# Hybrid decoder layer on one core: feed-forward operands stored as sums, three up products run in the output projection's phase, one DVE addition moved

## Chip, core and metric
One core of a Trainium2 chip runs the whole layer in one launch. The metric is device time in microseconds (us) of that launch; the median of several runs is compared. Everything is float32, and every large matmul is computed as three matmuls on operands split into a high and a low part (fp32r).

## What is computed
`x` is (1, 2048, 1024). The token-mixing half comes first (RWKV-7 recurrence and causal pooling); its result is `mixed_in`, and the change begins at its output projection. Cut to what matters:

```python
mixed = mixed_in @ w_out                              # 1024 x 1024
x = x + rms_norm(mixed, post_mix_norm)
h = rms_norm(x, pre_ffn_norm)
up = h @ w_up                                         # 1024 x 5632
up = causal depthwise conv over time (width 3) + conv_b
gate, val = split(up, 2)
f = (gelu_tanh(gate) * val) @ w_down                  # 2816 x 1024
x = x + rms_norm(f, post_ffn_norm)
```

## The kernel before
The kernel has four phases, one after the other, each a block with its own program for the five engines: input projection, recurrence, output projection (`phase_mix_out`, L1804) and feed-forward (`phase_ffn`, L2101). At the end of a phase all engines meet; a small block that sets semaphores (`credit`) stands between two.

**The products.** Up and down projection are multiplied by Strassen's method in Winograd's form: the operand is cut in four quarters, A11 to A22, four sums S1 to S4 are made of them, and seven products P1 to P7 replace eight. P1 is `ph` 0, P7 is `ph` 6. Of the eight quarters and sums seven are operands (`OPERANDS`); `OPERAND` is their place in memory. Each product of one weight tile is 4 x 3 = 12 matmuls (`split_matmul`, L130: L132, L133, L134).

**Output projection.** Sixteen tiles of 128 rows, written out (`tiles`). TensorE does tile t's 48 matmuls and then the eight transposes of tile t-1 (L2078). For each tile ScalarE squares the result (L1979), DVE scales it (L2050) and adds it to x (L2054), ScalarE squares x, DVE takes a reciprocal, ScalarE writes `xs` (L1992), which TensorE turns. DVE's `turn` (L2014) puts the turned tile into `quarter`; two tiles give one set of quarters, and `sums` (L2028) makes S1 to S4. ScalarE copies quarters and sums to high parts (L1952, L1959), GpSimd (L1927) and DVE (L2043) subtract them to get the low parts, and ScalarE's queue stores both parts in the memory tensors `q_hi` and `q_lo` (L1954, L1961, L1965, L1969). SyncE (SP) loads the mixed tiles and x, and behind the last tile the first three operands of the first superblock (L1910, L1911).

**Feed-forward.** Two superblocks of 1024 rows. In each, 22 units (one 128-wide gate tile and one value tile each) do the up projection. Units 0, 1, 20 and 21 are written out, the others are a hardware loop over pairs. In unit n ScalarE and DVE also split the weights of unit n+1 (`high` L2482, `low` L2638); GpSimd makes the weight sums `tsum` (`sums` L2415: L2425, L2427, L2430, L2434), in the first superblock also sums of down weights (`piece_sums` L2436), and sums of the hidden values of two units (`pair_sums` L2448, first line L2452), which wait for the hidden values (`hidden` L2670: DVE's product of gate and value, L2680). PSUM has four banks a unit; `BANK` says which product uses which, P4 goes onto P1's bank (after ScalarE's copy, L2494) and P7 onto P5's, after DVE's addition `add(n, 2, 4, ...)` (L2649 is the line of all additions). The order of DVE's steps in a unit is that of `unit` (L2722); in it `hidden(n - 1)` stands just ahead of `add(n, 2, 4, ...)`.

Then come 77 steps of the down projection (`step`), a ring of three buffers, split by L2533 (ScalarE) and L2684 (DVE). In the first superblock's steps SP also loads the next superblock's operands, high and low, in 56 parts. At the start of the phase SP loads the convolution parameters (L2348 to L2350), two weight tiles (L2291), operands 3 to 6 in high and low parts (L2310) and the last norm's gain (L2358).

Of the kernel before, what the change touches and what calls it, by code (L numbers as in the profile page):

```python
# [14 lines left out]
P = 128  # L15
# [33 lines left out]
OPERAND = (0, 4, 3, 1, 5, 6, 2)  # L49
EARLY_OPERANDS = 3  # L50

# [1752 lines left out]
def phase_mix_out(nc, a, scr):  # L1804
    ctx, sems = ExitStack(), []
    with ctx:
# [17 lines left out]
        m_lo = [scr["m_lo0"], scr["m_lo1"]]  # L1824
        x = two("x", [P, D_MODEL])
        hs = [sb("hs", [P, D_MODEL])] * 2
        xs = two("xs", [P, D_MODEL])
        sq = [sb("sq", [P, D_MODEL], mybir.dt.bfloat16)] * 2

        quarter = sb("quarter", [P, 8, KQ, P])  # L1830
        q_hi = sb("q_hi", [P, OPERANDS, KQ, P], F32R)
        q_lo = sb("q_lo", [P, OPERANDS, KQ, P], F32R)
# [25 lines left out]
        s_hh = sem("quarters_hi_ready")  # L1858
        s_hle = sem("first_quarters_lo_ready")
        s_hll = sem("last_quarters_lo_ready")  # L1860
        s_she = sem("first_quarters_hi_stored")
        s_shl = sem("last_quarters_hi_stored")
        s_sle = sem("first_quarters_lo_stored")
        s_sll = sem("last_quarters_lo_stored")
        s_pre = sem("first_operands_loaded")

        xv = a["x"][0].rearrange("(t p) d -> t p d", p=P)

# [9 lines left out]
        def place_of(q):  # L1878

            at = q // 4 * TB + q % 4 * P  # L1880
            return slice(at, at + P)

        credit(nc, sems)
        with nc.Block() as block:
            @block.sync
            def _(sp):
# [8 lines left out]

                def body(t, p):
# [8 lines left out]
                    if t == N - 1:  # L1905

                        for s in (s_she, s_shl, s_sle, s_sll):
                            sp.wait_ge(s, ONE + N // 4 * 16)
                        for ph in range(EARLY_OPERANDS):
                            sp.dma_start(scr["o_hi"][ph][:, :, :].bitcast(F32), scr["q_hi"][:, OPERAND[ph], :, 0:TB]).then_inc(s_pre, 16)  # L1910
                            sp.dma_start(scr["o_lo"][ph][:, :, :].bitcast(F32), scr["q_lo"][:, OPERAND[ph], :, 0:TB]).then_inc(s_pre, 16)  # L1911

                tiles(body)
                sp.wait_ge(s_pre, ONE + 32 * EARLY_OPERANDS)
                for p in range(2):
                    sp.wait_ge(s_sx[p], ONE + N * 8)
                for s in (s_she, s_shl, s_sle, s_sll):
                    sp.wait_ge(s, ONE + N // 2 * 16)

            @block.gpsimd  # L1920
            def _(gp):
                nc.gpsimd.memset(eps[:, :], NORM_EPS).then_inc(s_const, 1)

                def first_low(q):
                    gp.wait_ge(s_hh, ONE + 2 * q + 1)
                    gp.wait_ge(s_sle, ONE + q * 16)
                    nc.gpsimd.tensor_tensor(q_lo[:, 0:2, :, :], quarter[:, 0:2, :, :], q_hi[:, 0:2, :, :].bitcast(F32), ALU.subtract).then_inc(s_hle, 1)  # L1927

                def body(t, p):
                    if t < N - 2:  # L1930
                        gp.wait_ge(s_mh, ONE + t + 3)
                        nc.gpsimd.tensor_tensor(m_lo[p][:, :, :], m_raw[p][:, :, :], m_hi[p][:, :, :].bitcast(F32), ALU.subtract).then_inc(s_ml, 1)
                    if p == 1:
                        first_low(t // 2)


                gp.wait_ge(s_ml, ONE + 2)
                tiles(body)

            @block.scalar  # L1940
            def _(act):
# [6 lines left out]
                def first_high(q):  # L1948

                    act.wait_ge(s_h, ONE + 2 * q + 1)  # L1950
                    act.wait_ge(s_she, ONE + q * 16)
                    nc.scalar.activation(q_hi[:, 0:2, :, :], quarter[:, 0:2, :, :], ACT.Copy).then_inc(s_hh, 1)  # L1952
                    act.wait_ge(s_hh, ONE + 2 * q + 1)
                    act.dma_start(scr["q_hi"][:, 0:2, :, place_of(q)], q_hi[:, 0:2, :, :].bitcast(F32)).then_inc(s_she, 16)  # L1954

                def last_high(q):
                    act.wait_ge(s_sum, ONE + 4 * q + 4)
                    act.wait_ge(s_shl, ONE + q * 16)
                    nc.scalar.activation(q_hi[:, 2:OPERANDS, :, :], quarter[:, 3:8, :, :], ACT.Copy).then_inc(s_hh, 1)  # L1959
                    act.wait_ge(s_hh, ONE + 2 * q + 2)  # L1960
                    act.dma_start(scr["q_hi"][:, 2:OPERANDS, :, place_of(q)], q_hi[:, 2:OPERANDS, :, :].bitcast(F32)).then_inc(s_shl, 16)  # L1961

                def store_first_low(q):
                    act.wait_ge(s_hle, ONE + q + 1)
                    act.dma_start(scr["q_lo"][:, 0:2, :, place_of(q)], q_lo[:, 0:2, :, :].bitcast(F32)).then_inc(s_sle, 16)  # L1965

                def store_last_low(q):
                    act.wait_ge(s_hll, ONE + q + 1)
                    act.dma_start(scr["q_lo"][:, 2:OPERANDS, :, place_of(q)], q_lo[:, 2:OPERANDS, :, :].bitcast(F32)).then_inc(s_sll, 16)  # L1969

# [4 lines left out]
                def body(t, p):  # L1975
# [3 lines left out]
                    nc.scalar.activation(sq[p][:, :], bank[:, 2 * p:2 * p + 2, :].rearrange("p b d -> p (b d)"), ACT.Square,  # L1979
# [6 lines left out]
                    nc.scalar.activation(sq[p][:, :], x[p][:, :], ACT.Square, accum_out=ss[p][:, 1:2]).then_inc(s_sq, 1)  # L1986
# [3 lines left out]
                    if t > 1:  # L1990
                        act.wait_ge(s_tr, ONE + t - 1)
# [973 lines left out]
```

## Time and profile before

| | us |
|---|---|
| median of 3 runs | 2506.18 (2500.35 to 2506.23) |
| the profiled execution | 2502.93 |
| its span | 2499.8 |
| TensorE busy in the span | 2260.9 (90%) |
| DVE busy | 1730.0 (69%) |
| ScalarE busy | 1143.1 (46%) |
| GpSimd busy | 1007.0 (40%) |

The profile is of one execution. PE is TensorE's matmuls, PEld its weight loads, ACT ScalarE, POOL GpSimd, SP SyncE; a q behind a name is the engine's own sequencer, as where it issues a DMA. "Idle before, releaser" is the time an engine stood still before an instruction, and what it was released by. Matmuls overlap in their records: one of 512 columns is listed with 0.39 us, while the next starts sooner. The output projection runs from about 871 to 1094 us of the span, the first superblock from 1099 to 1816, the second to the end.

### The profile page before, as it was taken

The numbers are of one execution on the slowest core, as the hardware profiler recorded it, in microseconds if no ns is written. First come the engines' busy times: TensorE is split into PE (matmuls) and PEld (weight loads), VectorE is DVE, ScalarE is ACT, GpSimd is POOL, SyncE is SP. The second block draws the span as 40 slices with busy tenths as digits, with TensorE's granted clock in tenths as the row PEclk, the third lists the DMA queues.
The fourth block names the chain that finished last, engine by engine and source line by source line (L and its number), as shares of the span: only waits on it lengthen the run. The fifth ranks groups of instructions, "written<-read, shape, count | busy, mean of one in ns | idle before, by whom it ended". The sixth has DMA issues, their size and how long they took to land.

```text
span 2499.8 us, 44176 instructions
## 1 busy us (share of the span) xinstructions
PE 2260.9 (90%) x16652; PEld 1828.6 (73%) x16652; DVE 1730.0 (69%) x1869; ACT 1143.1 (46%) x1766; POOL 1007.0 (40%) x734
## 2 busy tenths in 40 slices
PE   6999999978899799828898998899989999999997
PEld 5786877757778678727777777788768787787885
DVE  2666797966865657547777777644688888885456
ACT  4657464623455545423443443344444444444434
POOL 4645464642233323225657576300045464541000
PEclk9999999998999999959999999999989999999999
DMA  6373645455566379995334444598743232325666
GB/s 181 96 233 118 225 127 189 124 181 154 159 189 181 88 219 284 292 289 191 127 128 144 134 155 134 168 308 289 270 134 106 84 105 88 105 81 198 193 219 209
DMA packets 481765, 431.16 MB, mean 172 GB/s; under 512 B 60444, under 2 KB 387788, under 8 KB 478796
## 3 DMA queue, kind: packets, MB, share of 16 engines
q1 hardware_dynamic: 395900, 349.35, 44.6%
q10 hardware_dynamic: 85712, 79.70, 9.9%
q8 instruction: 105, 1.72, 0.3%
q14 instruction: 48, 0.39, 0.1%
HBM read 284.79 MB, written 144.18 MB: 172 GB/s over the span
## 4 chain that ended last, share of the span: by engine, by line
PE 25%; DVE 10%; issue 10%; POOL 6%; DMA 2%; ACT 2%; SPq 1%; POOLq 0%; DVEq 0%; ACTq 0%
PE late_bank L132 9%; PE late_bank L134 8%; PE late_bank L133 8%; DVE p_wt_lo L2640 3%; DVE p_conv_gate L2662 1%; DVE p_conv_gate L2667 1%; DVE conv_val L2662 1%; POOL p_tsum L2434 1%; DVE p_ub L2649 1%; ACT p_wt_hi L2490 1%; DVE p_keep L2680 1%; POOL p_keep L2442 1%; POOL p_keep L2454 1%; POOL p_tsum L2427 1%; SPq L2310 1%
## 5 line engine op out<-in xcount | busy, mean ns | idle before, releaser
L132 PE MATMUL late_bank<-o_hi,p_wt_hi 128*128 128x512 f32 x1232 | 491.8, 399 | 103.6 <-DVE p_ub L2649 60.1
L133 PE MATMUL late_bank<-o_lo,p_wt_hi 128*128 128x512 f32 x1232 | 488.7, 397 | 0.0
L134 PE MATMUL late_bank<-o_hi,p_wt_lo 128*128 128x512 f32 x1232 | 488.0, 396 | 0.0
L132 PEld LDWEIGHTS late_bank<-o_hi,p_wt_hi 128*128 128x128 f32 x1232 | 236.9, 192 | 164.3 <-DVE p_ub L2649 57.9
L425 POOL TENSOR_TENSOR p_w_lo<-p_w_raw,p_w_hi 128x1024 fp32r<-128x1024 f32 x72 | 189.3, 2630 | 222.3 <-ACT p_w_hi L493 222.3
L134 PEld LDWEIGHTS late_bank<-o_hi,p_wt_lo 128*128 128x128 f32 x1232 | 236.7, 192 | 50.5
L133 PEld LDWEIGHTS late_bank<-o_lo,p_wt_hi 128*128 128x128 f32 x1232 | 236.8, 192 | 49.0
L132 PE MATMUL late_bank<-p_wt_hi 128*128 128x512 f32 x616 | 241.6, 392 | 12.7 <-DVE p_wt_lo L2684 11.4
L134 PE MATMUL late_bank<-p_wt_hi,p_wt_lo 128*128 128x512 f32 x616 | 240.4, 390 | 0.0
L133 PE MATMUL late_bank<-p_wt_lo,p_wt_hi 128*128 128x512 f32 x616 | 240.2, 390 | 0.0
L132 PE MATMUL p_ppr<-p_hT_hi,p_w_hi 128*128 128x512 f32 x576 | 233.2, 405 | 0.3 <-POOL p_w_lo L425 0.2
L134 PE MATMUL p_ppr<-p_hT_hi,p_w_lo 128*128 128x512 f32 x576 | 226.5, 393 | 0.0
L133 PE MATMUL p_ppr<-p_hT_lo,p_w_hi 128*128 128x512 f32 x576 | 226.2, 393 | 0.0
L2490 ACT ACTIVATE p_wt_hi<-p_tsum 128x512 fp32r<-128x512 f32 x176 | 109.4, 628 | 232.1 <-PE late_bank L134 166.1
L2684 DVE TENSOR_TENSOR p_wt_lo<-raw,p_wt_hi 128x1024 fp32r<-128x1024 f32 x104 | 130.7, 1256 | 117.8 <-ACT p_wt_hi L2533 117.4
L2649 DVE TENSOR_TENSOR p_ub<-late_bank,p_ub 128x512 f32<-128x512 f32 x220 | 150.7, 685 | 74.1 <-PE late_bank L134 72.3
L2640 DVE TENSOR_TENSOR p_wt_lo<-p_tsum,p_wt_hi 128x512 fp32r<-128x512 f32 x176 | 166.2, 945 | 37.4 <-ACT p_wt_hi L2490 37.4
L2640 DVE TENSOR_TENSOR p_wt_lo<-raw,p_wt_hi 128x512 fp32r<-128x512 f32 x132 | 135.3, 1025 | 77.3 <-ACT p_wt_hi L2490 77.2
L2533 ACT ACTIVATE p_wt_hi<-raw 128x1024 fp32r<-128x1024 f32 x104 | 110.2, 1060 | 149.6 <-PE late_bank L134 114.7
L2425 POOL TENSOR_TENSOR p_tsum<-raw 128x512 f32<-128x512 f32 x44 | 80.0, 1818 | 244.5 <-DMA out<-p_tsum 194.2
L132 PEld LDWEIGHTS late_bank<-p_wt_hi 128*128 128x128 f32 x616 | 115.8, 188 | 42.2 <-issue 14.2
L132 PEld LDWEIGHTS p_ppr<-p_hT_hi,p_w_hi 128*128 128x128 f32 x576 | 109.1, 189 | 36.6 <-issue 13.3
(298 smaller groups left out, 4580.5 us busy)
## 6 DMA issues: line engine op xcount, KB each, us to landing
raw<-in_w_up SPq DMA_DIRECT2D x88, 512.0 KB, 5.1
p_w_raw<-in_w_in SPq DMA_DIRECT2D x72, 512.0 KB, 3.9
scratch_a<-p_keep SPq DMA_DIRECT2D x22, 1280.0 KB, 6.2
raw<-scratch_a SPq DMA_DIRECT2D x104, 256.0 KB, 3.0
p_keep<-in_w_down SPq DMA_DIRECT2D x66, 256.0 KB, 3.2
raw<-scratch_td SPq DMA_DIRECT2D x60, 256.0 KB, 3.8
p_keep<-scratch_a SPq DMA_DIRECT2D x50, 256.0 KB, 2.9
scratch_td<-p_keep SPq DMA_DIRECT2D x22, 512.0 KB, 4.5
```

Source lines behind the costliest of these rows:

```text
L132: nc.tensor.matmul(out, lhs_hi, rhs_hi, start=start, stop=False, skip_group_check=again)
L133: nc.tensor.matmul(out, lhs_hi, rhs_lo, start=False, stop=False, skip_group_check=again)
L134: return nc.tensor.matmul(out, lhs_lo, rhs_hi, start=False, stop=stop, skip_group_check=again)
L425: nc.gpsimd.tensor_tensor(w_lo[i][:, :, :], w_raw[i][:, :, :], w_hi[i][:, :, :].bitcast(F32), ALU.subtract).then_inc(s_wl, 1)
L2310: sp.dma_start(dst[ph][:, :, :].bitcast(F32), scr[key][:, OPERAND[ph], :, sup * TB:(sup + 1) * TB]).then_inc(s_op[ph], 16)
L2425: nc.gpsimd.tensor_tensor(T1, B12, B11, ALU.subtract).then_inc(s_t, 1)
L2490: nc.scalar.activation(wt_hi[:, ph, :, :], weights(p, ph), ACT.Copy).then_inc(s_uh, 1)
L2533: nc.scalar.activation(dn_hi[r], dn_raw[r], ACT.Copy).then_inc(s_dh, 1)
L2640: nc.vector.tensor_tensor(wt_lo[:, ph, :, :], weights(p, ph), wt_hi[:, ph, :, :].bitcast(F32), ALU.subtract).then_inc(s_ul, 1)
L2649: nc.vector.tensor_tensor(dst, bank[:, b, :], src, ALU.add).then_inc(s_cd, 1)
L2662: nc.vector.scalar_tensor_tensor(cv[i][:, :], ub[p][:, i, 1:1 + WIDE], cpar[p][:, i, 1:2], cv[i][:, :], ALU.mult, ALU.add).then_inc(s_t1, 1)
L2684: nc.vector.tensor_tensor(dn_lo[r], dn_raw[r], dn_hi[r].bitcast(F32), ALU.subtract).then_inc(s_dl, 1)
```

## The change
- `phase_mix_out` no longer splits the feed-forward operands before it stores them. It stores the seven quarters and sums once, as float32, in a memory tensor `q`, from SP's queue, in one or two DMAs per set; S3 is made in A21's place. The operands of the first superblock's P1 to P3 are not stored: ScalarE and DVE split them straight into the feed-forward's buffers.
- `turn` now waits until the store of the previous set has landed. `hs`, `xs` and `sq` share one pair of buffers, `hx`.
- The split tensors `wt_hi`, `wt_lo` and `tsum` are allocated ahead of this phase. In it SP loads unit 0's and unit 1's weights, operands 3 to 6 as float32, parameters and gain; GpSimd makes unit 0's weight sums; ScalarE and DVE split unit 0's weights 0 to 2 within tile 14's step and weights and operands 3 and 4 after the last tile; TensorE runs P1 to P3 of unit 0 after the last tile's product, ahead of its transposes.
- `phase_ffn` splits what is left (`LATE`, 5 and 6) at its start, and skips unit 0's first three products. The next superblock's operands come in 28 parts as float32 and are split by ScalarE and DVE in every second down step, from step 12.
- The down steps are all written out, where most stood in hardware loops.
- In DVE's unit, `add(n, 2, 4, ...)`, which P7 waits for, stands ahead of `hidden(n - 1)`.

```diff
-OPERAND = (0, 4, 3, 1, 5, 6, 2)
+SLOT = (0, 5, 4, 1, 2, 6, 3)
...
+SUM_OF = {1: 1, 2: 0, 4: 2, 6: 3}
...
+        STORES = (((1, 4), (6, 7)), ((0, OPERANDS),))
+        HALF_Q = N // 4
...
+                def store_quarters(q):
+                    sp.wait_ge(s_sum, ONE + 4 * q + 4)
+                    for first, end in STORES[q // HALF_Q]:
+                        at = q % HALF_Q * P
+                        sp.dma_start(scr["q"][:, q // HALF_Q, first:end, :, at:at + P], quarter[:, first:end, :, :]).then_inc(s_qst, 16)
...
+                    if t > 2 and p:
+                        store_quarters((t - 3) // 2)
+
+                def begin_next():
+
+
+                    sp.wait_ge(s_mh, ONE + N)
+                    sp.wait_ge(s_ml, ONE + N)
+                    sp.wait_ge(s_op, ONE + N - 1)
+                    for i in range(2):
+                        sp.dma_start(raw[:, i, :, :], upv[:, i, :, 0:P]).then_inc(s_next["ur"][0], 16)
+                    sp.wait_ge(s_op, ONE + N)
+                    for ph in range(EARLY_OPERANDS, OPERANDS):
+                        sp.dma_start(o_lo[ph][:, :, :].bitcast(F32), scr["q"][:, 0, SLOT[ph], :, :]).then_inc(s_next["op"][ph], 16)
...
                 tiles(body)
-                sp.wait_ge(s_pre, ONE + 32 * EARLY_OPERANDS)
+                begin_next()
+                store_quarters(N // 2 - 1)
...
+                    for ph in range(EARLY_OPERANDS):
+                        nc.scalar.activation(o_hi[ph][:, :, q * P:q * P + P], quarter[:, SLOT[ph], :, :], ACT.Copy).then_inc(s_qh, 1)
...
+                    if 0 < t <= N // 2 and p == 0:
+                        first_high(t // 2 - 1)
+                    if t == N - 2:
+                        for ph in range(EARLY_OPERANDS):
+                            unit_high(ph)
 
                 tiles(body)
...
+                for ph in (3, 4):
+                    unit_high(ph)
+                    operand_high(ph)
...
                     if q > 0:
-                        dve.wait_ge(s_hh, ONE + 2 * q)
-                        dve.wait_ge(s_hle, ONE + q)
                         dve.wait_ge(s_sum, ONE + 4 * q)
-                        if p:
-                            dve.wait_ge(s_hll, ONE + q)
+                        dve.wait_ge(s_qst, ONE + stored(q))
+                        dve.wait_ge(s_qh, ONE + EARLY_OPERANDS * min(q, HALF_Q))
+                        dve.wait_ge(s_ql, ONE + EARLY_OPERANDS * min(q, HALF_Q))
...
+                    if 2 < t <= N // 2 + 1 and p:
+                        first_low((t - 3) // 2)
+                    if t > 0 and p:
                         turn(t - 1, 1 - p)
                     dve.wait_ge(s_rt, ONE + t * 2 + 2)
                     nc.vector.reciprocal(rt[p][:, 3:4], rt[p][:, 1:2]).then_inc(s_rc, 1)
                     if t > 0 and p == 0:
+                        turn(t - 1, 1 - p)
                         sums(t // 2 - 1)
-                    if t > 1 and p == 1:
-                        last_low(t // 2 - 1)
+                    if t == N - 2:
+                        for ph in range(EARLY_OPERANDS):
+                            unit_low(ph)
...
+                def early_product(ph):
+
+
+                    pe.wait_ge(s_ql, ONE + EARLY_OPERANDS * HALF_Q)
+                    pe.wait_ge(s_next["uh"], ph + 1)
+                    pe.wait_ge(s_next["ul"], ph + 1)
+                    pe.wait_ge(s_nm, ONE + (N if ph == 2 else N - 1))
...
                 tiles(body)
+                for ph in range(EARLY_OPERANDS):
+                    early_product(ph)
                 transposes(N - 1, 1)
...
+                    if c > 1:
+                        sp.wait_ge(s_ol, ONE + PH - EARLY_OPERANDS + c - 1)
+                    sp.dma_start(o_lo[ph][:, k, :].bitcast(F32), scr["q"][:, sup, SLOT[ph], k, :]).then_inc(s_oc[c % 2], 16)
...
-                        for ph in range(PH):
+                        for ph in LATE:
                             high(0, 0, ph)
+                            act.wait_ge(s_op[ph], ONE + 16)
+                            nc.scalar.activation(o_hi[ph][:, :, :], o_lo[ph][:, :, :].bitcast(F32), ACT.Copy).then_inc(s_oh, 1)
                         act.wait_ge(s_cw, ONE + 1)
...
                         low(n + 1, q, 3)
+                    add(n, 2, 4, c22(p), 4 * p + 3, c12(p))
                     if old:
                         hidden(n - 1, q, second(u) and sup)
-                    add(n, 2, 4, c22(p), 4 * p + 3, c12(p))
...
                 def unit(n, u, p, sup, f):
                     for ph in range(PH):
-                        product(n, u, p, ph, sup)
+                        if not begins(n) or ph >= EARLY_OPERANDS:
+                            product(n, u, p, ph, sup)
```

## Rows read from the trace of the kernel before

**Rows 1.** The page, costliest groups: line, engine, operation, tiles, count, busy, idle before, releaser.

```profile
L132 PE MATMUL late_bank<-o_hi,p_wt_hi 128*128 128x512 f32 x1232 | 491.8, 399 | 103.6 <-DVE p_ub L2649 60.1
```

**Rows 2.** Waits of TensorE: us, times, longest; stretches 860:1100, 1100:1600, 1840:2320.

```profile
PE late_bank L2078 <- ACT p_xs L1992: 25.0, 5, 18.8
...
PE late_bank L132 <- DVE p_ub L2649: 40.2, 11, 4.2
PE late_bank L132 <- DVE p_wt_lo L2640: 33.3, 1, 33.3
...
PE late_bank L132 <- DVE p_ub L2649: 19.9, 11, 3.0
```

**Rows 3.** Timeline at the end of the output projection: start, us, instruction, idle before.

```profile
1041.99 1.09 PE L2078 MATMUL late_bank<-p_ident,p_xs 128*128 128x128 f32 x8 [0.80 <-ACT p_xs L1992]
...
1054.27 12.10 ACTq L1961 DMA_DIRECT2D scratch_q_hi<-p_q_hi  x1
1066.47 1.02 ACT L1979 ACTIVATE p_sq<-late_bank 128x1024 bf16<-128x1024 f32 x1 [12.23 <-issue]
...
1073.62 1.97 PE L2078 MATMUL late_bank<-p_ident,p_xs 128*128 128x128 f32 x8 [18.76 <-ACT p_xs L1992]
...
1079.12 0.69 DVE L2038 TENSOR_TENSOR p_quarter<-p_quarter 128x512 f32<-128x512 f32 x1
```

**Rows 4.** Busy time by window: TensorE, weight loads, DVE, ScalarE, GpSimd, clock, DMA, GB/s.

```profile
1091.00:1094.00 3.00, 0.00 (x0) 0.00 (x0) 0.00 (x0) 0.00 (x0) 0.00 (x0) 0.50 1.00 287
1094.00:1097.00 3.00, 0.00 (x0) 0.00 (x0) 0.00 (x0) 0.00 (x0) 0.00 (x0) 0.50 0.03 8
```

**Rows 5.** The eight stores of L1961 (1280 KB each), from issue to landing.

```profile
DMA to landing us min/median/max: 6.5/10.3/20.6
```

**Rows 6.** Groups by shape in 990:1300, columns as in rows 1.

```profile
L2054 DVE TENSOR_TENSOR p_x<-p_x,p_hs 128x1024 f32<-128x1024 f32 x7 | 17.2, 2461 | 0.2
...
L2043 DVE TENSOR_TENSOR p_q_lo<-p_quarter,p_q_hi 128x2560 fp32r<-128x2560 f32 x5 | 14.1, 2824 | 5.6 <-DMA scratch_q_lo<-p_q_lo 5.6
...
L1959 ACT ACTIVATE p_q_hi<-p_quarter 128x2560 fp32r<-128x2560 f32 x4 | 9.4, 2342 | 9.5 <-DVE p_quarter L2038 9.5
```

**Rows 7.** Timeline at the start of the feed-forward.

```profile
1099.07 1.15 SPq L2348 DMA_DIRECT2D p_conv_gate<-in_conv_w  x3
...
1106.97 0.63 ACT L2490 ACTIVATE p_wt_hi<-raw 128x512 fp32r<-128x512 f32 x1 [24.79 <-DMA raw<-in_w_up]
...
1120.18 0.47 PE L132 MATMUL late_bank<-o_hi,p_wt_hi 128*128 128x512 f32 x1
...
1154.83 0.53 PE L132 MATMUL late_bank<-o_hi,p_wt_hi 128*128 128x512 f32 x1 [2.50 <-DVE p_ub L2649]
```

**Rows 8.** Timeline of one pair of units in the first superblock, by engine.

```profile
1417.65 0.59 PE L132 MATMUL late_bank<-o_hi,p_wt_hi 128*128 128x512 f32 x1 [3.88 <-DVE p_ub L2649]
...
1436.61 1.30 POOL L2452 TENSOR_TENSOR p_keep<-p_keep 128x512 f32<-128x512 f32 x1 [10.52 <-DVE p_keep L2680]
...
1450.98 1.16 ACT L2490 ACTIVATE p_wt_hi<-p_tsum 128x512 fp32r<-128x512 f32 x2 [5.79 <-POOL p_tsum L2427]
...
1459.09 1.58 DVE L2680 TENSOR_TENSOR p_keep<-p_conv_gate,conv_val 128x1024 f32<-128x1024 f32 x1
...
1461.33 0.50 PE L132 MATMUL late_bank<-o_hi,p_wt_hi 128*128 128x512 f32 x1 [3.68 <-DVE p_ub L2649]
```

**Rows 9.** Timeline of a unit of the second superblock.

```profile
1901.26 2.31 DVE L2680 TENSOR_TENSOR p_keep<-p_conv_gate,conv_val 128x1024 f32<-128x1024 f32 x1
...
1904.22 0.50 PE L132 MATMUL late_bank<-o_hi,p_wt_hi 128*128 128x512 f32 x1 [1.64 <-DVE p_ub L2649]
```

**Rows 10.** Waits in 1640:1790, down steps of the first superblock: us, times, longest.

```profile
ACT p_wt_hi L2533 <- PE late_bank L134: 73.4, 45, 1.8
DVE p_wt_lo L2684 <- ACT p_wt_hi L2533: 72.6, 51, 3.0
```

## What the change does to the time: the prediction

> **What bounds the kernel now.** First the page: TensorE is the engine to feed, and the largest group of its matmuls had 103.6 us of idle time before it, 60.1 of them put down to the DVE additions of L2649 [rows 1]. A busy share of 90% doesn't say where such time lies, so the waits of TensorE by stage come next [rows 2]. Three places stand out. (a) The seam between the output projection and the up projection: 18.8 us for `xs` of the last tile, then 33.3 us for the first split weights; both are single waits. (b) The up loop of the first superblock: 40.2 us in 11 waits for L2649. (c) The same loop of the second: 19.9 us in 11, 3.0 of them in its opening unit. Everywhere else TensorE is back to back: one product of a tile has 48 matmuls, and between the transposes at 1041.99 and the end of TensorE's work at 1073.62 - 18.76 = 1054.86 lie 12.87 us, two sets of transposes at 1.0 among them, so 0.2265 us a matmul and 2.72 us for a product of twelve [rows 3].
>
> At the seam the timeline tells who is late. Tile 15's product ends at 1053.8, but ScalarE sits 12.10 us in one store issue (q_hi, 1054.27) and starts tile 15's square at 1066.47; its transposes run at 1073.62, the last sum ends at 1079.81 [rows 3]. Then the stores drain: 287 GB/s up to 1094, 8 GB/s after it [rows 4]. Some 4.9 us later the next phase begins with parameters, then weights, which ScalarE has at 1106.97; P4 starts at 1120.18, P7 of unit 1 at 1154.83 [rows 7].
>
> **The change part by part.** I give instants on the clock of the profiled execution. E14 and E15 are the ends of the products of tiles 14 and 15, 1041.2 and 1053.8.
>
> *Tile loop.* ScalarE loses the 128x2560 copy of 2.34 us and five of its six store kinds, DVE the 128x2560 subtraction of 2.82, GpSimd the first low part [rows 6]. Per pair of tiles the stores fall from 3.7 MB to 1.0 (first eight tiles) or 1.8. TensorE waited for `xs` 25.0 us in five waits, of which 18.8 is the seam and 4.0 the first tile: 2.2 us could be won here [rows 2]. Against it stands a new wait: `turn` of an even tile overwrites `quarter`, so it waits until the store of the previous quarters has landed, and behind it on DVE stand the reciprocal, hence `xs`, hence the transposes. Square to transposes takes 7.15 us at the last tile [rows 3]; within the loop the x addition of L2054 averages 2.46 us [rows 6], beside GpSimd, which has nothing left to do at tile 15; I add 1.7 for it (an estimate). The sums then end 12.0 us after the product, DVE reaches the next `turn` 18 us after it, and TensorE wants `xs` at 23.8 with 2.6 us of work in between. So a store may take 9 us at no cost. Its bounds: 6.5 to 20.6 us for 1280 KB [rows 5], or 1.84 MB at 287 GB/s (6.4 us) plus about 2 of latency, 8.4 [rows 4]. I take 8.4, because the landings of rows 5 were measured under twice the traffic. The loop is worth 0, between -2 and +16.
>
> *Seam, first half.* The sums of tiles 12 and 13 end at E14 + 12.0 = 1053.2. SP then issues the 1.84 MB store and behind it 1.05 MB of weights: 10.1 us at 287 GB/s plus 2, weights at 1065.4; the bound below is the 5.9 us that the same load took with the queue empty (from five short issues after 1099.07 to 1106.97) [rows 7], that above 1.84 MB at the median pace of rows 5. ScalarE is parked in unit_high meanwhile, and DVE in unit_low, both ahead of tile 15: this replaces the 12.10 us issue. T1 and T2 take 1.44 us each (ten GpSimd operations between 1436.61 and 1450.98 [rows 8]), the two copies 0.6 each: square of tile 15 at 1069.6, 3.1 us later than now. Products 1 to 3 lie within that wait and behind it (8.2 us, with a slow start about 10), and P3 needs only the norm of tile 15. Transposes at 1076.7, sums done 6.2 later, 1082.9. One 1.84 MB store is left, landing at 1091.4 against 1094.2: only 2.8 us are won, although ScalarE, DVE and GpSimd do far less. The Trainium skill ("DMA: Bandwidth & Descriptors", Specifications) gives 512 B as the size from which transfers run at line rate; these stores have 512 B rows, and the trace shows 287 GB/s, so by that rule's about 436 GB/s the estimate for the last store would be 2.2 us shorter; I stay with the rows.
>
> *Seam, second half.* The new phase starts 4.9 us after the landing, at 1096.3. P1 to P3 are done. P4 accumulates onto P1's bank, so it needs P1's copy, which ScalarE makes only after the late weights and operands (LATE: 5, 6) and the taps. ScalarE: twice 0.63 [rows 7] and a 128x2048 copy, 2.34 x 2048/2560 = 1.9 [rows 6]: 5.1 us. DVE's last subtractions follow (2.3 each by the same scaling of 2.82), then taps, parameters and copy: P4 about 9.5 us after the start, at 1105.8 instead of 1120.18. From there ten products, P4 to P7 and P1 to P6, plus 2.0 us of half clock, bring P7 of unit 1 to 1135.0 instead of 1154.83: the operand and weight loads that delayed it have landed before. That is 19.8 us. The 2.50 us idle before it disappears, and with it the half clock after an idle: period 43.68 minus 14 products (38.05) minus the wait 3.68 leaves 1.9 us per stall [rows 8]. **Seam: 21.7 us**, between 10 and 27.
>
> *P7's addition, first superblock.* Before, the product of the even unit's hidden values (1459.09, 1.58 us) stood ahead of the addition that P7 waits for; without it P7 starts 1.5 us sooner. But there is a ring here: hidden values of the odd unit -> GpSimd, idle 10.52 us for exactly them at 1436.61 -> ten operations -> ScalarE, idle 5.79 us for L2427 at 1450.98 -> DVE -> P7 at 1461.33. The same edit holds back the other hidden product: it now stands behind an addition that needs P5. P5 ends 18.3 us after P7 restarted (1417.65; 2.72 + 1.9 + 5 x 2.72), add 0.68 and 1.23 for the product: 1437.9 instead of 1436.6 [rows 8]. 1.5 won, 1.3 given back. **2 us** over ten pairs, between -5 and +16.
>
> *Second superblock.* No piece sums, so GpSimd is early there and the ring is slack by about 1.6 us. The wait is 1.65, the hidden product ahead of the addition 2.31 [rows 9]: the wait goes. (19.9 - 3.0) = 16.9 us at most; TensorE is then back to back. GpSimd's pair sums start 1.3 us later and so reach over one more DVE tap. The Trainium skill ("SBUF — State Buffer", Who interferes with whom) says a DVE instruction with two SBUF inputs and a GpSimd one block each other for a whole instruction, which would put up to 1 us back into each pair. The rows have 2.31 against 1.58 for one operation [rows 8, 9], so I leave 0.2 in each pair. **15 us**, between 8 and 17.
>
> *Down stage of the first superblock.* 28 operand parts are now copied by ScalarE (0.63) and subtracted by DVE (2.82 x 512/2560 = 0.56, or up to 1.1 beside GpSimd), one in two steps of 2.72 us. ScalarE stood idle 73.4 us in 45 steps, DVE 72.6 in 51 [rows 10]: cover of 1.4 us or more a step. SP now waits for a part's low half ahead of the next step's load, about 1 us late, and half the bytes are gone. 0, at worst 28 x 0.2 = 6. The unrolled steps change no work: 0. If the cover were gone, each part would cost its 1.7 us.
>
> **Sum.** 0 + 21.7 + 2 + 15 = 38.7. The profiled execution took 2502.93 us with a span of 2499.8, 3.25 below the median 2506.18. Span 2461, that execution 2464, median **2467**.
>
> **The rivals.**
> *Stores pace the seam.* At the median pace of rows 5 a 1.84 MB store takes 14.7 us: weights and last store each 6 later, and three turns (tiles 11, 13, 15) lose 5: 27 us, 2494. For it: one queue, all loads of the next phase in front of the last store. Against it: the traffic that made that median is halved.
> *Both loops run free.* If the first superblock's ring is looser than I read it, ten times 1.5 us come on top: 2452. Against it: GpSimd's 10.52 us idle on the hidden product.
> *Slower.* `turn`, at each of its seven overwrites, waits for a store that takes the 20.6 us of rows 5: 20.6 + 12.1 + 2.6 - 23.8 = 11.5 us on TensorE, seven times 80, and 12 at the last store: 2559. It decides from a landing of about 14 us in every pair (7 x 5 us eat the gain). For it: 1.84 MB against 1.31. Against it: 1.0 MB in the first half, and SP's quiet queue.
>
> **How the numbers follow.** Forecast 0.62, both loops free 0.15, stores pace the seam 0.14, slower 0.05, an unseen wait that eats the gain 0.04. Range 2442 to 2492, from the free loops with a better seam to nearly the slow stores. This kernel's measurement can tell about 0.3% (7.5 us) from nothing: faster 0.92, same 0.04, slower 0.04.
>
> **What would show it.** Seam: TensorE's two waits become one of about 12 us ahead of P1 and one of about 27 ahead of P4; ScalarE's wait for the weights ends near 1065; first phase-4 instruction near 1096. First superblock: a wait of 3.5 us still at every second P7, its period 43.5, GpSimd's idle ahead of the pair sums about 12. Second: no wait at L2649, period 38.4 instead of 40.03. It is wrong if the wait in the first superblock vanishes, or if `xs` shows waits of several us at tiles 11, 13, 15.

## The result, and the profile after

The changed kernel takes **2536.55 us** (median of 4 runs, 2528.99 to 2538.19); the kernel before, on the same chip, 2503.5 (4 runs, 2500.35 to 2506.23). The ratio is 1.0122, 95% interval 1.01 to 1.0144: 1.2% slower, where 2467 was forecast. The profiled execution took 2538.19 us with a span of 2536.3.

Three instants cut the span so that each cause has a segment of its own: the start of tile 13's transposes (1041.99 before, [rows 3]; 1040.25 after), the first matmul of the down stage, and the first product of the second superblock. All are starts of instructions in TensorE's timeline.

| us | up to tile 13's transposes | from there to the down stage | down stage, first superblock | the rest | span |
|---|---|---|---|---|---|
| before | 1042.0 | 553.1 | 225.9 | 678.8 | 2499.8 |
| after | 1040.3 | 531.4 | **297.9** | 666.7 | 2536.3 |
| difference | -1.7 | -21.7 | **+72.0** | -12.1 | +36.5 |

Up to about 871 us the change touches nothing; the first segment differs by up to 9.4 us between the profiled executions here. The second and the last are the gains that were forecast. The loss lies in the down stage of the first superblock, for which the forecast had 0, at worst 6; it is about twice the gains.

TensorE's waits of the changed kernel (columns as in rows 2), in 860:1112, which answers to the first row of [rows 2]:

```profile
PE late_bank L2896 <- PEq L125: 16.7, 1, 16.7
PE late_bank L134 <- DVE wt_lo L2070: 11.7, 1, 11.7
PE late_bank L134 <- ACT p_ub L2517: 9.6, 1, 9.6
PE late_bank L2115 <- ACT p_hx L2021: 5.6, 1, 5.6
```

The 18.8 and 33.3 us of the old seam are three waits of 38.0 together. In the up loop of the first superblock (1112:1575), then in 1869:2350, the second superblock:

```profile
PE late_bank L134 <- DVE p_ub L2680: 33.7, 9, 4.0
...
PE late_bank L134 <- DVE p_ub L2680: 7.6, 10, 3.0
```

40.2 in 11 became 33.7 in 9, and 19.9 became 7.6 [rows 2]. The new item is in the down steps, where TensorE hardly waited before. The waits of all engines in 1620:1820, and of SP's queue:

```profile
DVE wt_lo L2715 <- ACT wt_hi L2556: 118.1, 26, 7.0
PEld late_bank L134 <- issue: 54.8, 26, 4.6
ACT wt_hi L2556 <- DMA raw<-scratch_td: 53.8, 11, 6.3
PE late_bank L134 <- DVE wt_lo L2715: 41.5, 23, 4.3
ACT wt_hi L2556 <- DMA raw<-in_w_down: 38.0, 7, 7.4
...
SPq L2351 <- DVE o_lo L2720: 139.2, 24, 7.7
```

In [rows 10] ScalarE waited for TensorE, as an engine should that runs ahead of it. Now it waits for loads, TensorE waits for the split, and the last row says why the loads are late: SP's queue stood 139.2 us in the wait of L2351, for DVE's low half of an operand part. The windows (columns as in rows 4), first the kernel before in 1620:1800:

```profile
1620.00:1800.00 180.00, 178.70 (x788) 147.44 (x787) 94.00 (x87) 76.47 (x81) 0.03 (x1) 1.00 0.88 293
```

and the changed one in 1620:1830:

```profile
1620.00:1830.00 210.00, 161.40 (x622) 123.72 (x621) 83.47 (x90) 68.51 (x83) 0.00 (x0) 0.93 0.52 168
```

The DMA engines were busy 52% instead of 88%: nothing is short of bandwidth. It is latency, in a ring, that is in a circle of waits in which each step is held by the one before it. One turn of it, in the timeline of the changed kernel (columns as in rows 3):

```profile
1766.52 0.32 SPq L2351 DMA_DIRECT2D o_lo<-scratch_q  x1
1766.94 0.38 SPq L2341 DMA_DIRECT2D raw<-scratch_a  x1
1767.36 0.43 SPq L2344 DMA_DIRECT2D raw<-scratch_td  x1
...
1771.28 1.06 ACT L2556 ACTIVATE wt_hi<-raw 128x1024 fp32r<-128x1024 f32 x1 [5.17 <-DMA raw<-scratch_td]
...
1772.24 0.61 ACT L2579 ACTIVATE o_hi<-o_lo 128x512 fp32r<-128x512 f32 x1
1772.37 1.23 DVE L2715 TENSOR_TENSOR wt_lo<-raw,wt_hi 128x1024 fp32r<-128x1024 f32 x1 [4.74 <-ACT wt_hi L2556]
...
1773.51 0.68 DVE L2720 TENSOR_TENSOR o_lo<-o_lo,o_hi 128x512 fp32r<-128x512 f32 x1
1773.74 0.47 PE L134 MATMUL late_bank<-wt_hi 128*128 128x512 f32 x1 [2.01 <-DVE wt_lo L2715]
...
1774.22 0.32 SPq L2351 DMA_DIRECT2D o_lo<-scratch_q  x1
```

Read it as a circle. SP issues a part, then the loads of the next two steps (0.84 us to the second load of the first step). The weights are there 3.92 us later, at 1771.28. ScalarE splits them, 1.09; DVE splits them and, behind that in its order, makes the low half of the operand part that had been loaded long ago, 1.82, up to 1774.19. SP, which waits for just this low half, issues the next part at 1774.22, and only then the next two steps' loads. 0.84 + 3.92 + 1.09 + 1.82 + 0.03 = **7.70 us** for two steps, whose 24 matmuls need 24 x 0.2265 = 5.44. The part's data is not late anywhere; its wait stands in SP's queue ahead of step loads, and its release stands in DVE's order behind a split that needs those loads.

Over the stage: between the second part's issue at 1606.70 and the last at 1821.92 lie 26 turns, 8.28 us each in the mean, 2.84 over the 5.44, in all 74 us against the 72.0 of the table. The turn shown is one of the shortest: all but the first (10.9) take 7.60 to 9.96. In the one of 9.96 the time from the load's issue to the copy is 6.18 (1666.94 to 1673.12) where it is 3.92 above, and the rest is the same.

### The profile page after: what moved, and what is told of

Read it like the earlier page. It is cut to its first block, busy times and chain, and to the rows that moved or that the text cites. A ratio compares the mean times of both kernels' runs of the same rounds, so it can differ in the third digit from the quotient of the medians.

```text
span 2536.3 us, 43637 instructions
## 1 busy us (share of the span) xinstructions
PE 2288.2 (90%) x16652; PEld 1843.6 (73%) x16652; DVE 1743.5 (69%) x1905; ACT 1138.4 (45%) x1794; POOL 990.9 (39%) x726
## 3 DMA queue, kind: packets, MB, share of 16 engines
q8 instruction: 111, 1.82, 0.3%
## 4 chain that ended last, share of the span: by engine, by line
PE 19%; DVE 12%; issue 9%; POOL 7%; DMA 6%; ACT 3%; SPq 1%; POOLq 0%; ACTq 0%; DVEq 0%
PE late_bank L134 6%; PE late_bank L136 6%; PE late_bank L135 6%; DVE wt_lo L2671 2%; DMA raw<-scratch_td 2%; DMA raw<-in_w_down 2%; DVE wt_lo L2715 2%; DVE p_conv_gate L2693 2%; ACT wt_hi L2556 1%; DMA p_keep<-in_w_down 1%; POOL tsum L2456 1%; DVE conv_val L2693 1%; DVE conv_val L2698 1%; POOL p_keep L2462 1%; POOL p_keep L2466 1%
## 5 line engine op out<-in xcount | busy, mean ns | idle before, releaser
L134 PE MATMUL late_bank<-o_hi,wt_hi 128*128 128x512 f32 x1232 | 493.4, 400 | 68.6 <-DVE p_ub L2680 41.3
L135 PE MATMUL late_bank<-o_lo,wt_hi 128*128 128x512 f32 x1232 | 490.4, 398 | 0.0
L136 PE MATMUL late_bank<-o_hi,wt_lo 128*128 128x512 f32 x1232 | 489.5, 397 | 0.0
L134 PEld LDWEIGHTS late_bank<-o_hi,wt_hi 128*128 128x128 f32 x1232 | 238.3, 193 | 127.4 <-DVE p_ub L2680 45.9
L134 PE MATMUL late_bank<-wt_hi 128*128 128x512 f32 x616 | 250.4, 406 | 62.3 <-DVE wt_lo L2715 56.6
L136 PEld LDWEIGHTS late_bank<-o_hi,wt_lo 128*128 128x128 f32 x1232 | 237.8, 193 | 50.7
L135 PEld LDWEIGHTS late_bank<-o_lo,wt_hi 128*128 128x128 f32 x1232 | 238.1, 193 | 49.7
L136 PE MATMUL late_bank<-wt_hi,wt_lo 128*128 128x512 f32 x616 | 247.1, 401 | 0.0
L135 PE MATMUL late_bank<-wt_lo,wt_hi 128*128 128x512 f32 x616 | 246.9, 401 | 0.0
L2671 DVE TENSOR_TENSOR wt_lo<-tsum,wt_hi 128x512 fp32r<-128x512 f32 x173 | 154.3, 893 | 42.7 <-ACT wt_hi L2513 42.1
```

The source lines that it names most:

```text
L134: nc.tensor.matmul(out, lhs_hi, rhs_hi, start=start, stop=False, skip_group_check=again)
L135: nc.tensor.matmul(out, lhs_hi, rhs_lo, start=False, stop=False, skip_group_check=again)
L136: return nc.tensor.matmul(out, lhs_lo, rhs_hi, start=False, stop=stop, skip_group_check=again)
L2671: nc.vector.tensor_tensor(wt_lo[:, ph, :, :], weights(p, ph), wt_hi[:, ph, :, :].bitcast(F32), ALU.subtract).then_inc(s_ul, 1)
```

## Experiments

**Parts further apart.** The theory gives a repair: let the wait look four parts back, so that it never meets work that depends on what stands behind it.

```diff
-        s_oc = [sem(f"operand_part_loaded{i}") for i in range(2)]
+        s_oc = [sem(f"operand_part_loaded{i}") for i in range(4)]
...
-                    if c > 1:
-                        sp.wait_ge(s_ol, ONE + PH - EARLY_OPERANDS + c - 1)
+                    if c > 3:
+                        sp.wait_ge(s_ol, ONE + PH - EARLY_OPERANDS + c - 3)
```

(and `c % 4`, `c // 4` where the part is loaded and awaited.)

> The changed kernel, but SP's load of an operand part (down stage of the first superblock) has four semaphores in turn and waits for the low half of the part four before it, not two. Theory (a closed ring): SP waits for a low half that DVE makes only behind the split of the next down step, whose load SP issues only after that wait; two steps then take SP issue 1.2 + landing 4 + ScalarE 1.06 + DVE 1.9, some 7.8 us, where 24 matmuls take 5.44. With the wait opened the down stage falls from 286 us back to about 215 and the time to about 2468 us. Rival A (the added copies and subtractions of ScalarE and DVE, or the loads' landing, are the bound): nothing moves, 2536. Rival B (the written-out steps cost instruction fetch): nothing moves, 2536.

Measured: 2468.29 us (4 runs, 2459.6 to 2471.66; here and below, ratios are to the kernel before, run again beside each group of experiments), ratio 0.9855 (0.9826 to 0.9883). The waits of 1620:1780:

```profile
ACT wt_hi L2556 <- PE late_bank L136: 68.0, 49, 2.6
DVE wt_lo L2715 <- ACT wt_hi L2556: 56.9, 49, 2.0
...
PE late_bank L134 <- DVE wt_lo L2715: 1.9, 2, 1.4
```

and the window:

```profile
1620.00:1780.00 160.00, 158.15 (x697) 130.33 (x696) 101.42 (x108) 81.32 (x98) 0.00 (x0) 1.00 0.76 245
```

ScalarE waits for TensorE again, SP issues a part every 5.44 us in most turns, and the stage takes 228.4 us instead of 297.9. A wait that looks two parts further back, with two more semaphores, takes away 68 us of the time.

**One part more between.** Is it the ring, or does each semaphore only loosen a shortage? Here the wait looks three back (`c > 2`, `c - 2`, three semaphores), the smallest step.

> The changed kernel, where SP waits for the low half of the part three back instead of two back (three semaphores). Theory (a closed ring of 7.8 us through SP, the load of a step's weights, ScalarE and DVE stands against 5.44 us of matmuls in two steps): with one part more between, the ring's 7.8 us stand against 10.9 us of matmuls, so it no longer binds: 2468 us, as with four semaphores. Rival (the parts themselves are late, by the traffic or by ScalarE's and DVE's work, and each semaphore only gives some slack): halfway, about 2500 us.

Measured: 2465.95 us (4 runs), ratio 0.9848 (0.9833 to 0.9863), stage 229.0 us. One step is enough, as it must be where 7.70 us stand against 5.44 once and against 10.9 then; halfway was not seen.

**SP waits for the copy instead.** This shortens the ring by DVE's part and leaves it closed.

```diff
-                        sp.wait_ge(s_ol, ONE + PH - EARLY_OPERANDS + c - 1)
+                        sp.wait_ge(s_oh, ONE + PH - EARLY_OPERANDS + c - 1)
```

> The changed kernel, but SP waits for ScalarE's copy of the part two before, not for DVE's low half. The ring theory says that the ring gets shorter by what lies between the two ends, 1.3 to 1.4 us of some 7.8, so 27 rounds of two steps give 35 to 38 us: about 2500. It is still longer than 5.44 us, so the waits of TensorE don't go away. Rivals A and B: 2536, nothing moves.

Measured: 2502.41 us (10 runs), ratio 1.0 (0.9983 to 1.0017); stage 261.3 us. From the second part's issue at 1597.89 to the last at 1779.01 a turn is 6.97 us in the mean, 1.31 less than with the wait for the low half; 1.3 to 1.4 was expected. A shorter ring gives a shorter turn, and it still exceeds 5.44. Together the three runs show the ring.

**P7's addition alone.** The kernel before, with only `add(n, 2, 4, ...)` ahead of `hidden(n - 1)`.

```diff
+                    add(n, 2, 4, c22(p), 4 * p + 3, c12(p))
                     if old:
                         hidden(n - 1, q, second(u) and sup)
-                    add(n, 2, 4, c22(p), 4 * p + 3, c12(p))
```

> The kernel before with one edit: in DVE's unit the addition that P7 waits for stands ahead of the hidden product. Ring theory for the first superblock (hidden product of the odd unit, GpSimd's sums, ScalarE, DVE, P7): its wait stays, period 43.8 to 44.4, cost 0 to 6 us. Second superblock: the waits at the additions fall from 19.9 us to under 8, gain about 12. In all -6 to -12: 2492 to 2498. Rival (the addition was the bound in both): -30, 2474, with waits at the additions gone in both.

Measured: 2487.07 us (4 runs), ratio 0.9938 (0.992 to 0.9956), so 16 us won (11 to 20): more than I expected here, and about the 17 us that the prediction has for its two terms. The rest after the down stage is 667.1 us, 11.7 less than before; up to the down stage 9.6 are won, though the ring forecast there keeps its wait at the other units. TensorE's waits in 1100:1600 of this run, then those of 1565:1640, at the start of the down stage, first in the kernel before:

```profile
PE late_bank L132 <- DVE p_ub L2649: 32.7, 9, 4.0
```

```profile
PE late_bank L132 <- DVE p_wt_lo L2684: 4.4, 3, 2.1
```

```profile
PE late_bank L132 <- DVE p_wt_lo L2684: 6.6, 3, 4.4
```

The first row was 40.2 in 11 [rows 2]: 7.5 of the 9.6 us are waits. But the last of the eleven, 2.2 us at the end of the up loop, comes back behind it: 4.4 grew to 6.6, and the down stage takes 2.2 us more than before (228.1).

**Down steps written out, alone.** The kernel before without its loops over steps.

```diff
-                    with loop(0, (FP - 2) // RING) as g:
-                        for e in range(e0 + 1, e0 + 1 + RING):
-                            step(g * RING + e, g + e // RING, e % RING, ph, None, sup)
...
+                for e in range(STEPS):
+                    step(e, e // RING, e % RING, e // FP, e % FP, sup)
```

> The kernel before with all down steps written out instead of mostly in hardware loops, nothing else. Ring theory: 0, within 3 us. Rival B: the down stage of the first superblock gets longer by up to 70 us, and that of the second too.

Measured: 2503.67 us (10 runs), ratio 1.0001 (0.9985 to 1.0018). The down stage takes 225.7 us (225.9 before). The recorded 0 holds, and the slower stage isn't owed to the form of the code. The Trainium skill ("Runtime: NRT & Kernel Launch", Instruction fetch mechanics) says that a taken branch stalls for a fetch when its target lies outside the two pages at hand, and that kernels prefer full unrolling where possible for this reason, among others. No gain from unrolling shows here.

**The hidden product's place by unit.** On top of the four semaphores. The addition stays ahead in odd units of the first superblock; in even units, where the product is the odd unit's, for which GpSimd waits, it goes back ahead of the addition.

```diff
+                    if old and p == 0 and sup == 0:
+                        hidden(n - 1, q)
                     add(n, 2, 4, c22(p), 4 * p + 3, c12(p))
-                    if old:
+                    if old and not (p == 0 and sup == 0):
                         hidden(n - 1, q, second(u) and sup)
```

> The changed kernel with four semaphores for the operand parts (2468 us), and in the first superblock's even units the hidden product stands ahead of P7's addition again; the odd units keep the new order. Ring theory (the first superblock's ten waits of 3.7 us are held by a ring: hidden values of the odd unit, GpSimd's sums, ScalarE's copy, DVE's low part, P7): the new order helps only where it takes the hidden product from ahead of the addition that P7 waits for, and in the other unit it holds GpSimd back by 1.3 us. Each pair of units gets 1.3 us shorter if that reading is right, 9 pairs: 2468 - 12 = 2456 us, period of a pair 42.6 instead of 43.9 us, wait 2.4 instead of 3.7. Rival (the wait hangs on something other than GpSimd's start, such as DVE's own queue): no difference, 2468 us, or 1.5 us per pair lost, 2482 us, if the even unit's addition was the one that mattered.

Measured: 2439.72 us (4 runs, 2438.07 to 2444.33), ratio 0.9753 (0.9736 to 0.9769). It is 28.6 us below the kernel with four semaphores (26.2 below the one with three, whose runs stood beside these), where 12 were expected; in the two profiled executions 23.4 of it lie between tile 13's transposes and the down stage (527.2 to 503.9), 6.1 in the first segment, which the edit doesn't touch, and behind the up loop 0.2 is given back. GpSimd's idle ahead of the pair sums and TensorE's wait, first with four semaphores alone, then with the order by unit:

```profile
1369.98 1.69 POOL L2474 TENSOR_TENSOR p_keep<-p_keep 128x512 f32<-128x512 f32 x1 [11.73 <-DVE p_keep L2711]
...
1349.73 0.50 PE L134 MATMUL late_bank<-o_hi,wt_hi 128*128 128x512 f32 x1 [3.86 <-DVE p_ub L2680]
```

```profile
1308.28 1.29 POOL L2474 TENSOR_TENSOR p_keep<-p_keep 128x512 f32<-128x512 f32 x1 [8.97 <-DVE p_keep L2711]
...
1331.53 0.50 PE L134 MATMUL late_bank<-o_hi,wt_hi 128*128 128x512 f32 x1 [2.38 <-DVE p_ub L2680]
```

The wait fell by about 1.4, as expected of this ring. The surprise is a second gain of the same size: a pair took 43.9 us before the edit ((1525.96 - 1174.76) / 8, starts of P7 behind such waits) and 40.9 for most of the loop after it ((1413.30 - 1168.18) / 6). 40.9 is the 38.05 of fourteen products plus 2.4 of wait plus 0.4; 43.9 had 2.1 beyond its wait. The granted clock says where that was, first in four semaphores' 1220:1350, then in this kernel's 1250:1410:

```profile
1220.00:1350.00 130.00, 118.90 (x503) 97.11 (x502) 101.81 (x102) 52.89 (x84) 85.89 (x61) 0.96 0.43 139
```

```profile
1250.00:1410.00 160.00, 152.61 (x670) 125.49 (x670) 137.25 (x134) 68.17 (x110) 112.35 (x78) 1.00 0.46 151
```

With four semaphores the clock fell to its lower level for a time behind eight of the nine waits, of 3.0 to 3.9 us (mean 0.96; 0.94 over 1200:1560); with the order by unit it stayed at the upper one behind the first six, of 2.3 to 2.7 (1.00). The length of the wait alone doesn't decide it. With four semaphores the pair behind the wait of 3.54 us at 1307.47 ran at the upper level throughout and took 42.26 us, and with the order by unit the clock fell behind the wait of 2.67 us at 1413.30 (0.57 over 1412:1420), and that pair took 43.34:

```profile
1307.00:1349.00 42.00, 38.40 (x168) 31.45 (x168) 34.73 (x35) 17.24 (x29) 28.81 (x21) 1.00 0.44 144
```

```profile
1412.00:1420.00 8.00, 6.70 (x17) 5.29 (x18) 6.83 (x8) 3.86 (x6) 6.73 (x5) 0.57 0.20 62
```

So the second gain is there where the rows show the upper level, but no run changes the clock without the wait.

**Weights first.** Four semaphores, and `load_weights()`, the first loads of `begin_next`, moved ahead of the store of tiles 12 and 13 on SP.

```diff
                     sp.dma_start(x[p][:, :], xv[tile(t)]).then_inc(s_x[p], 16)
+                    if t == N - 1:
+                        load_weights()
                     if t > 2 and p:
                         store_quarters((t - 3) // 2)
```

> The changed kernel with four semaphores for the operand parts (2468 us), and the load of unit 0's up weights issued on SP ahead of the store of tiles 12 and 13, at the end of product 14. Theory (ScalarE and DVE are parked for these weights, 15.1 us, which lie behind the store): the weights arrive 6 us sooner, the square of tile 15 stands 6 us earlier, TensorE's 11.7 us wait for P1 falls to 6 or less; but the last store is then still behind all the loads, so that the phase ends only about 4 us earlier: 2464 us. Rival (what ends the phase is the chain over the last tile alone): all 6 to 10 us come through, 2459 us. Rival (the last store is bound by the 7 MB of loads ahead of it on the same queue): nothing comes through, 2468 us.

Measured: 2462.07 us (4 runs, 2456.78 to 2466.81), ratio 0.9833 (0.9813 to 0.9854). By the time alone this can't be told from four semaphores (2459.6 to 2471.66), nor one forecast from the others; the trace tells them apart. ScalarE's 15.15 us wait for the weights is gone and TensorE's 11.8 ahead of P1 is down to 1.4, yet the one at the meeting of the engines grew from 16.8 to 25.0, and P4 starts only 2.9 us sooner (59.8 us behind tile 13's transposes instead of 62.7). The last store is issued 5.6 us sooner, at 1076.17, but stands behind 5.9 MB of loads: all engines meet 3 us sooner. The instants fit the first theory, which had 4 us.

**All of it, and the rest of the seam.** The two edits above; the last store ahead of the loads of operands 5 and 6; and LATE's splits behind the copy of P1 on ScalarE, and behind the taps (the coefficients of the convolution) on DVE.

```diff
+                        if ph == EARLY_OPERANDS + 1:
+                            store_quarters(N // 2 - 1)
...
-                store_quarters(N // 2 - 1)
...
+                    if begins(n):
+                        for ph in LATE:
+                            high(0, 0, ph)
+                            act.wait_ge(s_op[ph], ONE + 16)
+                            nc.scalar.activation(o_hi[ph][:, :, :], o_lo[ph][:, :, :].bitcast(F32), ACT.Copy).then_inc(s_oh, 1)
```

> Both of the above together, and in the seam the last store moved ahead of the loads of operands 5 and 6, and in unit 0 of the feed-forward the splits of the late weights and operands moved behind P1's copy on ScalarE and DVE, so that P4 doesn't wait for them. If the terms add: 2468 - 12 (hidden product) - 4 (weights first) - 5 (late splits, of which ScalarE has 5.1 us ahead of P1's copy) - 3 (store ahead of two loads of 2 MB) = 2444 us. If P4 only moves its wait to P6, whose operands are then late: 2449 us. If the first superblock's ring doesn't move: 2456 us.

Measured: **2430.64 us** (5 runs, 2422.29 to 2438.95), ratio to before 0.9716 (0.9691 to 0.9742), the fastest of all. Its seam, TensorE's and SP's rows:

```profile
1035.86 1.03 PE L2120 MATMUL late_bank<-p_ident,p_hx 128*128 128x128 f32 x8
...
1064.38 0.38 SPq L1906 DMA_DIRECT2D scratch_q<-p_quarter  x1
...
1082.96 0.62 PE L2904 MATMUL late_bank<-conv_val 44*128 44x44 f32 x4 [22.65 <-PEq L125]
1084.90 0.77 PE L134 MATMUL late_bank<-o_hi,wt_hi 128*128 128x512 f32 x1 [1.32 <-ACT p_ub L2522]
1094.76 0.47 PE L134 MATMUL late_bank<-o_hi,wt_hi 128*128 128x512 f32 x1 [2.33 <-DVE p_ub L2686]
```

P4 comes 49.0 us behind tile 13's transposes, 13.7 less than in the two kernels that keep the seam; its wait fell from 9.6 to 1.3. Of these 13.7, 9.5 are left at the down stage (494.3 against 503.9): the splits that were moved are in the way of unit 0's P7 (2.33) and later steps. Of the 13.7, 2.9 were there with the weights first; the rest can't be shared out between the store's place and the splits, which came in one run. By adding terms 2444 was expected; with the 28.6 us of the order by unit in place of the 12 it would have been 2428, near the measured time.

The segments of the profiled executions of all experiments:

| us | to tile 13's transposes | to the down stage | down stage | the rest | span |
|---|---|---|---|---|---|
| four semaphores | 1042.1 | 527.2 | 228.4 | 667.8 | 2465.5 |
| three semaphores | 1045.3 | 524.7 | 229.0 | 666.9 | 2465.9 |
| SP waits for the copy | 1039.8 | 525.6 | 261.3 | 667.4 | 2494.0 |
| down steps written out | 1040.8 | 556.7 | 225.7 | 678.2 | 2501.3 |
| addition alone | 1039.7 | 543.6 | 228.1 | 667.1 | 2478.4 |
| hidden product by unit | 1036.0 | 503.9 | 230.5 | 665.9 | 2436.2 |
| weights first | 1042.1 | 523.2 | 229.3 | 667.3 | 2461.7 |
| all | 1035.9 | 494.3 | 228.4 | 668.0 | 2426.6 |

## Why the prediction was wrong

**The step that failed is the down stage of the first superblock**: "SP now waits for a part's low half ahead of the next step's load, about 1 us late ... 0, at worst 28 x 0.2 = 6". It measured 72.0 us. The wait was seen, its place ahead of the step's load too; the lateness was reckoned once, with everything around it on time. What the working left out is that the late load comes back: DVE makes the next low half behind a split that needs it. A wait that closes a ring isn't priced by its lateness but by the ring's length against the work it holds. All terms of that length stood in the trace of before: two issues, the landing of a load (in its 1620:1800, from issue, median)

```profile
raw<-scratch_td SPq DMA_DIRECT2D x29, 256.0 KB, 4.0
```

a copy, a split, and the part's 0.56 to 1.1. That is 0.8 + 4.0 + 1.1 + 1.2 + 0.6 = 7.7 against 5.44, 26 times 2.3: 59 us, with the sign and most of the size; the mean turn was 8.28. The signs that the prediction named for being wrong lay in other stages, and none of them came: the wait in the first superblock stayed, and `xs` had no waits at tiles 11, 13 and 15. "Half the bytes are gone" was no help either. The same loads in the changed kernel, 1620:1820:

```profile
raw<-scratch_td SPq DMA_DIRECT2D x18, 256.0 KB, 4.4
```

At 168 GB/s instead of 293 they land no sooner. By the Trainium skill ("SBUF — State Buffer", The DMA setup-cost knee) a transfer pays about 2 us whatever its size, and its fit gives an estimate of 2.6 us for one of 256 KB. The rows, of a queue with other loads in it, lie above that with 4.0 and 4.4.

With the wait moved two parts back the stage costs 228.4 us, 0.3 more than in the kernel with the addition alone, which has no such parts: the *work* of the parts is worth 0, as the recorded cover of 1.4 us a step has it. The kernel with four semaphores takes 2468.29 us, where 2467 was forecast for this change. That it comes so close is in part luck: the misses below, in both directions, offset each other.

The other steps, by that kernel or by the changed one:

- *Tile loop*, 0: right. DVE's new wait shows as 5.3 us in two (longest 2.8) up to 1080, and TensorE has no wait for `hx` but the first tile's 5.6. The slower rival put the loss here, at 11.5 us in every turn; the slower result came from another wait, so that this rival wasn't borne out. (The 14.7 us of a 1.84 MB store at the median pace of rows 5 should read 14.4: the store is 1792 KB, and 10.3 x 1792 / 1280 = 14.4. It changes no forecast.)
- *Seam*, 21.7: right in its instants. Counted from tile 13's transposes, which come 1.7 us sooner, weights were expected at 1063.7 and ScalarE has them at 1062.69; the square of tile 15 at 1067.9, it starts at 1066.77; the last store at 1081.2, it is issued at 1080.26; P4 at 1104.1, it starts at 1103.11:

```profile
1062.69 0.63 ACT L1996 ACTIVATE wt_hi<-raw 128x512 fp32r<-128x512 f32 x1 [15.13 <-DMA raw<-in_w_up]
...
1066.77 1.00 ACT L2010 ACTIVATE p_hx<-late_bank 128x1024 f32<-128x1024 f32 x1
...
1080.26 0.37 SPq L1906 DMA_DIRECT2D scratch_q<-p_quarter  x1
```

  Before, P4 came 78.2 us behind the transposes, now 62.9. The difference between four semaphores and the addition alone, which is the seam by itself, is 16.4 us up to the down stage: a quarter less than 21.7. The addition alone removes the early wait at unit 1's P7 too, so that this wait (2.50, and 1.9 of half clock) must not be counted for both; 17.3 is left to compare. The -21.7 of the first table is the same number by chance: it holds this term and the next.
- *P7's addition, first superblock*, 2: the mechanism was right, the size not. The wait of 3.6 to 4.0 us stands at every second P7, as written, and GpSimd's idle grew from 10.52 [rows 8] to some 11.8. The period of a pair was 44.3 us in the changed kernel ((1528.39 - 1173.95) / 8), where 43.5 was forecast. But the addition alone won 9.6 us up to the down stage: two of the eleven waits vanish (2.50 at unit 1, 2.22 at the end), the nine left are shorter by 2.8 together, and the 2 us that remain may be the clock's, which no run here shows by itself. The down stage gives 2.2 back. That half of the edit won and half gave back is what the order by unit shows: with the good half alone 23.4 us more come.
- *Second superblock*, 15: the wait goes from one of its ten pairs in full and from nine all but 0.5 us in each, the period is 38.9 instead of 40.03 (38.4 was forecast), and 12.1 us are won (10.8 to 12.9 in the other kernels). Near the estimate, a little below.
- *Down steps written out*, 0: right.

Without the failed term the sum would be some 34 us of span less by four semaphores (0.1, -25.9, +2.5 and -11.0 by segment), beside the forecast 38.7.

## What to carry to other kernels

When a change puts a wait into a queue, follow what is queued behind it until you come back to the work that ends the wait. If you come back, add up the circle, issues and landing times included, and compare it with the work that it is allowed to hide behind: here 7.7 us against 5.44, 26 times. One more semaphore in the circle, which cost nothing here, doubles what it is compared with (10.9 us instead of 5.44; the stage fell from 297.9 to 229.0); and of a reordering that helps one unit and hurts the next, take the half that helps.

## What was not expected of the hardware

- The clock came with a small difference of a wait and made a large one of it: with waits of 3.4 to 3.9 us in each pair its mean was 0.94 to 0.96, with waits of 2.3 to 2.7 it was 1.00 over 160 us, and there a pair was 3.0 us shorter for a wait shorter by 1.4. The length alone doesn't decide it: the clock fell behind one of 2.67 us and stayed up behind one of 3.54.
- Loads of 256 KB took 4.4 us (median) with the DMA engines 52% busy at 168 GB/s, 4.0 with 88% at 293, and 3.1 in the kernel with four semaphores at 245: latency did not follow traffic.
- SP's queue can stand in an issue (changed kernel): two weight loads behind a pending 1.84 MB store took it 6.04 us (L1927), two behind the operands 8.20 (L1942), where a free issue takes 0.32 to 0.43.
- The same code ahead of the seam differed by up to 9.4 us between profiled executions (1035.9 to 1045.3), so a gain of a few us must be read from a segment and not from the span.
